# Up-projection weights with eight neighbouring rows per partition in a streaming-encoder step, and gathered tokens turned every eighth column

## The reference

```python
def _hier_moe(xn, lp):
    ...
    e_ids = g_sel[:, None] * EXPERTS_PER_GROUP + top_i
    combine = jnp.sum(jax.nn.one_hot(e_ids, N_EXPERTS, dtype=f32) * w_sel[..., None], axis=1)
    y = jnp.zeros((n, D_MODEL), f32)
    for e in range(N_EXPERTS):
        h = jax.nn.silu(xt @ lp['w1'][e]) * (xt @ lp['w3'][e])
        y = y + combine[:, e:e + 1] * (h @ lp['w2'][e]).astype(f32)
    return y.astype(xn.dtype).reshape(shp)
```

## Time and profile before

| what | value |
|---|---|
| runs | 1275.93 us median, 1274.86 to 1277.11 |
| profiled execution | 1274.02 us |
| its span, first to last instruction | 1271.9 us |
| PE busy in the span | 1104.5 us (87%) |
| weight loads of the expert stage | 96 of 1 MB, median 16.0 us from issue to landing |
| queue that SP issues to | 178.56 MB, 42.1% of the time of 16 DMA engines |

### The profile page before, as it was taken

One profiled execution on the slowest core, in us unless ns is written; L12 is line 12 of the kernel. 1 busy time (PEld: TensorE's weight loads), 2 busy tenths in 40 slices (PEclk: granted clock), 3 DMA queues, 4 the chain that ended last, 5 costly groups with the idle time before them and its releaser, 6 DMA issues. The chain is left out here.

```text
span 1271.9 us, 19333 instructions
## 1 busy us (share of the span) xinstructions
PE 1104.5 (87%) x6920; PEld 808.8 (64%) x6920; DVE 508.6 (40%) x999; ACT 269.2 (21%) x598; POOL 363.7 (29%) x222
## 2 busy tenths in 40 slices
PE   1799999999989997799989999981899999999760
PEld 1698888889888886699979994551333333333210
DVE  5425778486848666730042111116111111111116
ACT  2123333324232433511120001120000000000002
POOL 3352451516151510365646650000010011011003
PEclk9999999899999998899989999995899999999995
DMA  5351242514233220242262217902999785289966
GB/s 173 92 176 55 67 136 65 152 49 128 76 101 107 68 76 1 67 132 82 66 232 66 77 43 261 353 34 67 359 379 373 268 293 172 75 289 374 381 231 247
DMA packets 186293, 204.81 MB, mean 161 GB/s; under 512 B 13527, under 2 KB 132311, under 8 KB 186214
## 3 DMA queue, kind: packets, MB, share of 16 engines
q1 hardware_dynamic: 176678, 178.56, 42.1%
q0 software_dynamic: 3760, 12.85, 3.3%
q10 hardware_dynamic: 5776, 12.32, 2.9%
HBM read 180.56 MB, written 22.95 MB: 160 GB/s over the span
## 5 line engine op out<-in xcount | busy, mean ns | idle before, releaser
L1682 PE MATMUL bank<-wbuf,on 128*64 128x512 f32 x864 | 200.5, 607 | 16.3 <-DMA wbuf<-in_w 14.7
L176 POOL TENSOR_TENSOR wh<-raw,zcol 128x1024 fp32r<-128x1024 f32 x40 | 77.3, 1932 | 272.8 <-DMA raw<-in_w_in 218.2
L1682 PEld LDWEIGHTS bank<-wbuf,on 128*64 128x64 f32 x864 | 61.2, 139 | 132.1 <-issue 119.5
L599 PE MATMUL bank<-xh,wh 128*128 128x320 f32 x384 | 122.4, 319 | 0.0
L600 PE MATMUL bank<-xl,wh 128*128 128x320 f32 x384 | 119.1, 310 | 0.0
L601 PE MATMUL bank<-xh,wl 128*128 128x320 f32 x384 | 119.1, 310 | 0.0
L1708 PE MATMUL bank<-wbuf,on 128*64 128x512 f32 x432 | 98.7, 598 | 1.8 <-DVE on L1775 1.8
L179 POOL TENSOR_TENSOR wl<-raw,wh 128x1024 fp32r<-128x1024 f32 x40 | 99.3, 2482 | 3.1
L599 PE MATMUL bank<-wh,xh 128*128 128x256 f32 x320 | 93.4, 292 | 6.1 <-POOL wTp L582 6.1
L600 PE MATMUL bank<-wl,xh 128*128 128x256 f32 x320 | 90.3, 282 | 0.0
L601 PE MATMUL bank<-wh,xl 128*128 128x256 f32 x320 | 90.2, 282 | 0.0
(11 more groups left out here) (257 smaller groups left out, 2038.0 us busy)
## 6 DMA issues: line engine op xcount, KB each, us to landing
wbuf<-in_w SPq DMA_DIRECT2D x96, 1024.0 KB, 16.0
raw<-in_w_in SPq DMA_DIRECT2D x40, 512.0 KB, 4.9
kc<-in_cache_k SPq DMA_DIRECT2D x8, 1024.0 KB, 6.4
vc<-in_cache_v SPq DMA_DIRECT2D x8, 1024.0 KB, 5.5
wraw<-in_w_in SPq DMA_DIRECT2D x16, 512.0 KB, 3.6
block_outputs<-on ACTq DMA_DIRECT2D x54, 128.0 KB, 6.3
block_outputs<-zero ACTq DMA_DIRECT2D x9, 512.0 KB, 6.7
wraw<-in_w_attn_proj SPq DMA_DIRECT2D x8, 512.0 KB, 3.5
```

The source lines that it names most:

```text
L176: nc.gpsimd.tensor_tensor(wh[:, :, j, :], r[:, :, :], zcol[:, 0:1].rearrange("p (a b) -> p a b", a=1) .to_broadcast([P, KT, P]), ALU.add). ...
L599: nc.tensor.matmul(out, ah, bh, start=(k == 0), stop=False)
L1682: mm = nc.tensor.matmul(bank[2][B * j:B * (j + 1), 0:2 * FG].rearrange("p (i f) -> p i f", i=2), xT[:, t * B:(t + 1) * B], w[:, :, k, FG * ...
```

## The change

Three places are edited. The views `w1s` and `w3s` now put row p*8 + k into partition p, slice k. A partition thus holds eight neighbouring rows, and the four rows of one half lie side by side in memory: 8 KB. To match, slice k of the tokens is now every eighth column, beginning at column k, where before it was 128 neighbouring columns; the transposes read their stationary operand with a step of eight floats (32 bytes). The clearing of `xrows` at the start covers 1024 columns instead of 128, since the first transpose reads 128 partitions over the whole row. The down weights, the gather, all sums and all other instructions stay.

```diff
-    w1s = A["w1"][0].rearrange("e (k p) f -> e p k f", p=P)
-    w3s = A["w3"][0].rearrange("e (k p) f -> e p k f", p=P)
+    w1s = A["w1"][0].rearrange("e (p k) f -> e p k f", k=KT)
+    w3s = A["w3"][0].rearrange("e (p k) f -> e p k f", k=KT)
...
-            nc.gpsimd.memset(xrows[:, 0:P], 0.0).then_inc(rows_clear, 1)
+            nc.gpsimd.memset(xrows[:, :], 0.0).then_inc(rows_clear, 1)
...
             def turn_tokens(b):
                 pe.wait_ge(xg_in, b * 16 + 16)
-                nc.tensor.transpose(bank[0][:, 0:P], xrows[:, 0:P], ident)
+                by_k = xrows[:, :].rearrange("b (p k) -> b k p", k=KT)
+                nc.tensor.transpose(bank[0][:, 0:P], by_k[:, 0, :], ident)
                 for k in range(1, KT):
-                    mm = nc.tensor.transpose(bank[0][:, k * B:(k + 1) * B], xg[:, k * P:(k + 1) * P], ident[0:B, 0:B])
+                    mm = nc.tensor.transpose(bank[0][:, k * B:(k + 1) * B], by_k[0:B, k, :], ident[0:B, 0:B])
                 mm.then_inc(xt_done, 1)
```

## The result

The changed kernel takes 1284.13 us, the median of 4 runs (1283.14 to 1286.14), against 1276.05 us before (4 runs): a ratio of 1.0068 with a 95% interval of 1.0052 to 1.0084. That is 8.7 us (6.6 to 10.7) slower by the ratio; the medians lie 8.1 us apart. One of six runs of `turn_only` had a granted clock of 0.82 over the whole run instead of 0.95 and took 1363.96 us; it is left out of that kernel's numbers. The profiled execution takes 1283.14 us, its span 1281.1 us, 9.2 us more than before.

A forecast was written before the change was run, and what follows sets the result against it. PE's blocks bound the expert stage up to 1129.48 us, then a chain of DMA loads. Terms +0.75 - 4.1 + 8.4 + 1.0 = +6.05 us gave 1280.1 us profiled, 1282.0 us for the runs, range 1271 to 1289 us.

The forecast's parts named there:

- The likeliest case: Whole kernel: the stepped turn costs about what half rate costs, 1282.0 us, own range 1278 to 1286.5; chance 0.52.
- Which regime counts where: Expert stage: PE's time counts before SP's load at 1129.48 us, DMA time in the chain behind it.
- The turn: 21 turns on PE's path, each 0.40 us longer from the step of 32 bytes: +8.4 us, from 0 to +9.9.
- the seven later turns: Turns after the one at 1124.95 us: 2.8 us of added work, costing nothing while the loads end last.
- The rule that was cited: Stepped turn: a 16-byte SBUF line must be hit twice to hide the access, so the turn costs more; no factor given.
- The pieces: 8 KB pieces for 20 up loads in the chain behind 1129.48 us: -4.1 us, from 0 to about -4.8.
- the straight line: Up loads: 8.6 ns saved per piece between 2 and 4 KB, extended to 8 KB: 0.21 us per load.
- Clearing: Wider memset of xrows before the first gather, fully on the path while PE idles: +0.75 us.
- Gathers: Two of the first three turns get gathers late behind larger pieces: +0.5 us each, +1.0 us, bounds 0 and +2.
- the rival by which gathers become the bound: Between 916 and 1129 us about ten turns wait 2.5 us for gathers beside full loads: 1307 us; chance 0.07.
- a free step: Turn: stepped loads run at the rate of neighbours, so the kernel takes 1273.6 us, 1271 to 1278; chance 0.34.
- a quarter rate: Turn: each float fetched by itself, +1.28 us per turn, +26.9 us over 21 turns, 1300 us; chance 0.07.

The follow-up runs named there:

- turn_only: Turn read with a step of 32 bytes and wide clearing, weights still in 2 KB pieces, against the kernel before: 1283.59 us, ratio 1.0057.
- step2: Two neighbouring rows per partition, 4 KB pieces, turn reading every second column, clearing of 256 columns, against the kernel before: 1283.69 us, ratio 1.0059.
- the layout alone: Weight views in 8 KB pieces only, turn and clearing as before, against the kernel before: 1275.42 us, ratio 0.9990.
- before_again: The kernel before, unchanged, run once more for a second trace: 1279.01 us in one run.

## Why the prediction was right

The forecast was 1282.0 us, slower; the runs show 1284.13 us. The likeliest case was the one that came. The runs show its path and its two opposite terms; how near single terms came is in part luck, as told below.

**Which regime counts where: right.** The stepped turn cost time in the blocks that PE bounds and the pieces gained time in the chain behind SP's load, as the sum had it.

**The turn: right, at 7.6 instead of 8.4 us.** It was put at 0.40 us and measured 0.382 (the period's growth over 18 blocks). Of the 21 turns in the sum, 19 cost that. The first cost 0.03 us at the lower clock. The second is hidden: the third turn waits for its gather, and POOL issues this gather 2.22 us after the second turn starts, in both kernels, because its index column comes from VectorE, which is busy until then.

```profile
904.93 0.90 POOL L1648 DMA_INDIRECT on<-xn_scratch,idx  x1 [9.56 <-DVE idx L1765]
...
908.97 0.90 POOL L1648 DMA_INDIRECT on<-xn_scratch,idx  x1 [11.07 <-DVE idx L1766]
```

(First before, with the second turn at 902.71, then after, with that turn at 906.75.) Of the seven later turns, which the prediction put at nothing, the last one costs 0.37 us, since it lies behind the chain. So 19 x 0.382 + 0.37 = 7.6 us.

The reason given for the 0.40 was that the load is the fastest reader in the trace and loses when a fetch brings one useful float instead of several. The runs do not bear it out, so that the figure came so near is in part luck. The load is not the fastest reader: 62 ns for 128 columns are 0.48 ns each, while `up` streams 512 columns in 225 ns, 0.44 ns each (3.60 us for 16); the prediction's 0.65 ns took in the step to the next instruction. And the price does not follow how many useful floats a fetch could bring, for step2 pays as much as the change. A limit that does not go with the array's clock fits: stepped loads stand as far apart at a granted clock of 0.50 as at 1.00 (110 ns with a step of eight, about 120 with four or two), while neighbours stand 107 ns apart at 0.50 and 62 at 1.00 (first and later turns). The rule that was cited, the Trainium skill, "Advanced Engine Details and Errata", section "SBUF Cachelines", asks for two hits on a 16-byte line to hide the access; by it a step of two floats would run free, and the trace disagrees, with 215 ns against 139 (step2). Where in the path of a load the rate drops is not shown.

**The pieces: mechanism right, size too large.** The term was -4.1 us for the chain. It measured -3.2 (88.19 against 91.38 us), -2.9 with the layout alone; over all traces the mean is 88.26 us in five kernels with 8 KB pieces and 91.28 in four with 2 KB (90.57 to 91.81), 3.0 us. That is 0.15 us for each of 20 loads, where the straight line from the earlier trace rows gave 0.21; the 4 KB pieces alone gave 2.3 of it in the one trace that has them, so most of the saving seems to come from the first doubling. And not all of it reaches the end. From SP's load to PE's last instruction the means are 103.69 and 105.64 us, 1.95 us apart (traces with a stepped last turn stand in both groups). In all five 8 KB traces the last half of `up` took 5.35 us or more after a wait of 3.1 to 3.9 us (granted clock 0.67 in it after the change), in three of the four 2 KB traces 3.65 us after 0.25 to 2.59 us. I had counted that half at nothing, with a note that a shorter wait may spare 1.7 us. It went the other way, and the profile that I summed against was the one of four with the slow half.

**Clearing: +0.25 us at most instead of +0.75.** The wider memset takes the time of the row, but the gap behind it, which I left out, shrank, so the gather starts 0.40 us later. The first turn comes 0.25 us later, the lower clock taken off; against traces with that clock it is 0.04 us (126.20 against 126.16 with the layout alone) and 0.10 (126.03 with the turn alone against 125.93 in `before_again`).

**Gathers: +0.8 instead of +1.0 us, at one place instead of two.** Only the third turn waits longer, 0.96 us after 0.24. Its gather is issued at the same distance from the second turn, so the whole +0.83 us to the third turn is its landing, 8.3 us after issue instead of 7.5. Over the traces it lands after 7.8 to 8.5 us with 8 KB pieces, 7.6 with 4 KB and 7.3 to 7.5 with 2 KB, though the loads move the same bytes; from the second turn to the third it is 0.7 us longer on average (10.39 against 9.67 us). The second turn does not wait for its gather in either kernel. The 0.81 us in the earlier trace rows stand on PEld, which idles as long before this load in the middle blocks (13.0 us before 16 of them); PE's own row at 902.71 has no idle time. (POOL issues a gather when the turn of the block just before it is done, not two before, as the section on the kernel before has it: `gather(b)` waits for `b` turns.) Between 929 and 1136 us no turn waits for a gather, so the rival by which gathers become the bound is refuted, and so are the rivals of a free step and of a quarter rate.

**What is left.** By these terms the profile shows +0.25 + 7.63 + 0.83 - 3.19 = +5.5 us, and 3.75 us of the span's 9.2 were the execution's own (0.55 + 1.70 + 1.50); the two together account for the span. With the pieces' mean worth to PE's end, -1.95, the sum is +6.8 us, inside the interval of the runs (6.6 to 10.7), but 1.9 us below its middle of 8.7. It agrees with the parts: turn and clearing +7.9, measured 7.3 (4.5 to 10.1); layout -1.95 + 0.7 = -1.25, measured -1.3 (-2.8 to +0.3). Whether another 2 us or so belong to the change is open; no row that I found carries them, and ten traces are too few to tell whether it makes the lower clock in the first `up` more frequent.

## What to carry to other kernels

Price a new layout at every reader of the data, by how often it reads and what stands behind it: here larger DMA pieces were worth 2 us in the one stretch that the loads bound, and the step they forced was paid in every block that PE bounds. When an order must change, change it once, on an engine with time to spare, so that the repeated reader keeps neighbours. And take a second trace of the unchanged kernel before a difference of stretches is read as an effect: 3.2 us of this one came and went without any edit.

## What was not expected of the hardware

- A stationary load of 128 float32 columns on 64 partitions takes about the same at any step tried from 2 to 8 floats: 182 to 228 ns each (means by place) against 134 to 142 for neighbours, 91 to 129 ns apart against 57 to 65. There was no gradual slope up to 16 bytes.
- The stepped load is no slower at half the granted clock (110 ns apart at 0.50 and at 1.00 with a step of eight; neighbours 107 and 62), so its step costs next to nothing there.
- A gather among weight loads lands later when their pieces are larger, at the same bytes: 7.8 to 8.5 us after issue with 8 KB pieces, 7.3 to 7.5 with 2 KB (third gather of the stage).
- VectorE's operation on 1024 floats went from 1.28 us to 2.08 with a stepped read of both inputs and to 2.00 us with an output written at a step of 128 floats (512 bytes).
